# S5 convolution kernel products in four column groups of one PSUM bank, and their way to the Toeplitz matrices

## What is computed

```
dt = exp(log_dt);  a = exp(lambda*dt);  b' = ((a-1)/lambda) * b        # complex, per group and state
x[t] = a*x[t-1] + b' u[t]                                             # 512 tokens, an associative scan
y[t] = Re(c x[t]) + d_skip * u[t]
```

## Time and profile before

| what | value |
|---|---|
| median of 3 runs | 995.13 us (994.78 to 995.26) |
| the profiled execution, its own time | 994.91 us |
| span of its trace | 993.2 us |
| mean granted TensorE clock | 0.990 |

### The profile page before, as it was taken

One profiled execution on the slowest core, in us unless ns is written; L12 is line 12 of the kernel. 1 busy time (PEld: TensorE's weight loads), 2 busy tenths in 40 slices (PEclk: granted clock), 3 DMA queues, 4 the chain that ended last, 5 costly groups with the idle time before them and its releaser, 6 DMA issues.

```text
span 993.2 us, 14475 instructions
## 1 busy us (share of the span) xinstructions
PE 892.3 (90%) x4962; PEld 501.5 (50%) x4962; DVE 307.6 (31%) x812; ACT 173.9 (18%) x396; POOL 161.5 (16%) x260
## 2 busy tenths in 40 slices
PE   8999999999999999999979888988888887777865
PEld 3445876554444444445845555555555544343432
DVE  5990665761111111144731111111111111111117
ACT  1222148751000000100101111111111111111110
POOL 2010014430000000000022222222222222121210
PEclk9999999999999999999989999999999999999988
DMA  8342824029222220161799999999999999999555
GB/s 309 71 88 94 104 34 160 2 75 418 96 85 89 88 90 4 72 272 43 312 394 417 416 421 422 423 421 418 420 425 418 422 420 425 423 421 425 248 182 220
DMA packets 44553, 255.36 MB, mean 257 GB/s; under 512 B 15163, under 2 KB 15691, under 8 KB 28100
## 3 DMA queue, kind: packets, MB, share of 16 engines
q1 hardware_dynamic: 33988, 244.42, 62.2%
q0 software_dynamic: 10240, 9.64, 3.7%
q10 hardware_dynamic: 288, 0.81, 0.2%
HBM read 257.32 MB, written 21.04 MB: 280 GB/s over the span
## 4 chain that ended last, share of the span: by engine, by line
PE 63%; SPq 22%; DMA 6%; DVE 5%; issue 3%; ACT 1%; DVEq 0%; ACTq 0%; POOLq 0%
PE ps L665 19%; PE ps L804 9%; SPq L354 9%; SPq L347 8%; PE ps L443 6%; PE ps L701 6%; PE ps L824 5%; DMA reg_bo<-experts 4%; PE ps L435 3%; PE ps L622 2%; PE ps L578 2%; SPq L352 2%; PE ps L600 2%; PE ps L504 2%; SPq L411 1%
## 5 line engine op out<-in xcount | busy, mean ns | idle before, releaser
L804 PE MATMUL ps<-arena,reg_a 128*64 128x256 f32 x1024 | 118.2, 383 | 9.7 <-DMA arena<-experts 7.8
L1539 DVE TENSOR_TENSOR small<-reg_u,ps 128x128 f32<-128x128 f32 x62 | 17.9, 288 | 349.1 <-ACT reg_u L1050 349.1
L665 PE MATMUL ps<-xT,arena 128*128 128x512 f32 x256 | 111.2, 592 | 0.0
L804 PEld LDWEIGHTS ps<-arena,reg_a 128*64 128x64 f32 x1024 | 84.2, 138 | 52.4 <-issue 30.1
L1671 POOL DMA_INDIRECT ye_scratch<-reg_bo,reg_u x62 | 62.8, 1014 | 231.7 <-ACT reg_bo L1057 226.1
L665 PEld LDWEIGHTS ps<-xT,arena 128*128 128x128 f32 x256 | 48.6, 190 | 61.2 <-issue 61.2
L824 PE MATMUL ps<-arena,small 128*64 128x512 f32 x256 | 63.7, 616 | 13.8 <-DVE small L1546 13.0
L1057 ACT COPY reg_bo<-ps 128x512 f32<-128x512 f32 x62 | 36.4, 586 | 208.3 <-PE ps L824 208.3
L665 PE MATMUL ps<-reg_u,arena 128*128 128x512 f32 x128 | 57.5, 592 | 0.0
L701 PE MATMUL ps<-reg_a,reg_bo 128*128 128x512 f32 x128 | 55.8, 593 | 0.0
L443 PE MATMUL ps<-xT,reg_bo 128*128 128x512 f32 x128 | 55.7, 595 | 0.0
(11 more groups left out here) (277 smaller groups left out, 1155.7 us busy)
## 6 DMA issues: line engine op xcount, KB each, us to landing
arena<-experts SPq DMA_DIRECT2D x32, 2048.0 KB
arena<-experts SPq DMA_DIRECT2D x32, 1024.0 KB
reg_bo<-experts SPq DMA_DIRECT2D x8, 2048.0 KB
reg_a<-experts SPq DMA_DIRECT2D x8, 2048.0 KB
arena<-mid_w SPq DMA_DIRECT2D x8, 1792.0 KB, 7.4
xT<-experts SPq DMA_DIRECT2D x7, 2048.0 KB
x<-experts SPq DMA_DIRECT2D x7, 2048.0 KB
reg_bo<-experts SPq DMA_DIRECT2D x8, 1024.0 KB
```

The source lines that it names most:

```text
L665: m = pe.matmul(ps[bank][:, :], w[:, (o + c) * P:(o + c + 1) * P], rhs[:, c, :], start=(c == 0), stop=(c == nk - 1))
L804: m = pe.matmul(ps[2 + c % 2][64 * h:64 * h + 64, 0:DE], xgT[:, x, BLK * (c % 2):BLK * (c % 2 + 1)], gates[k][:, x * 512 + h * DE:x * 512 ...
```

## The change

The 16 pairs are taken four at a time (b = 0 to 3). The four pairs q = 0 to 3 of a batch write to partitions 32q to 32q+31 of bank 0, columns 128b to 128b+127, first the real parts of the four, then the imaginary parts. All 32 products end in one bank of 128 partitions by 512 columns. One count of s_kmm follows the last, ACT makes one copy to `kst`, now 128 partitions by 4 by 128, and DVE adds d_skip in a form of 128 partitions by 64 numbers, whose product is now made ahead of the wait. In `kst` each 16 partitions r hold the taps of groups r, r+8, r+16, r+24, so the taps go out by 8 transfers for each k, 64 in all, of 16 partitions times 4 groups.

```diff
-        kst = x1[0:32, 0:2048].rearrange("p (g n) -> p g n", g=GP)
+        kst = x1[:, 0:512].rearrange("p (b n) -> p b n", b=4)
...
-            sp_.wait_ge(s_kmm, 4)
+            sp_.wait_ge(s_kmm, 1)
...
-            sp_.wait_ge(s_kst, 5)
+            sp_.wait_ge(s_kst, 2)
             sp_.wait_ge(s_zero, 4)
             for k in range(T8):
-                for g2 in range(2):
-                    sp_.dma_start(toep[SH * k:SH * (k + 1), g2:SG:2, (T8 - 1 - k) * SH:P],
-                                  kst[SH * g2:SH * (g2 + 1), :, 0:(k + 1) * SH]).then_inc(s_toep, 16)
+                for r in range(8):
+                    sp_.dma_start(toep[SH * k:SH * (k + 1), r:SG:8, (T8 - 1 - k) * SH:P],
+                                  kst[SH * r:SH * (r + 1), :, 0:(k + 1) * SH]).then_inc(s_toep, 16)
...
-            for g in range(GP):
-                out = ps[g // 4][0:32, (g % 4) * P:(g % 4 + 1) * P]
-                pe.matmul(out, bbz[:, 0, g, :], ca_re[:, g, 0:8, :], start=True, stop=False)
-                m = pe.matmul(out, bbz[:, 1, g, :], ca_ni[:, g, 0:8, :], start=False, stop=True)
-                if g % 4 == 3:
-                    m.then_inc(s_kmm, 1)
+            for b in range(4):
+                for ri in range(2):
+                    for q in range(4):
+                        g = 4 * b + q
+                        m = pe.matmul(ps[0][32 * q:32 * q + 32, b * P:(b + 1) * P], bbz[:, ri, g, :], (ca_re, ca_ni)[ri][:, g, 0:8, :],
+                                      start=(b == 0 and ri == 0), stop=(ri == 1), skip_group_check=True)
+            m.then_inc(s_kmm, 1)
...
             pe.wait_ge(s_wv, 16)
+            pe.wait_ge(s_kst, 1)
             for t in range(TT):
-                pe.wait_ge(s_kst, t + 1)
...
-            pe.wait_ge(s_toep, 16 * 16)
+            pe.wait_ge(s_toep, 16 * 64)
...
-            for n in range(4):
-                act.wait_ge(s_kmm, n + 1)
-                act.copy(kst[:, 4 * n:4 * n + 4, :], ps[n][0:32, :].rearrange("p (q n) -> p q n", q=4)).then_inc(s_kst, 1)
+            act.wait_ge(s_kmm, 1)
+            act.copy(kst, ps[0][:, :].rearrange("p (b n) -> p b n", b=4)).then_inc(s_kst, 1)
...
-            dve.wait_ge(s_kst, 4)
-            sk = work[0:32, 0:256].rearrange("p (g h) -> p g h", g=GP)
-            link(tt(sk, s5d.unsqueeze(2).broadcast_to([32, GP, SH]), eyeh.unsqueeze(1).broadcast_to([32, GP, SH]), ALU.mult))
+            sk = work[:, 0:4 * SH].rearrange("p (b h) -> p b h", b=4)
+            link(tt(sk, s5d.unsqueeze(2).broadcast_to([P, 4, SH]), eyeh.unsqueeze(1).broadcast_to([P, 4, SH]), ALU.mult))
+            dve.wait_ge(s_kst, 1)
             dve.tensor_tensor(kst[:, :, 0:SH], kst[:, :, 0:SH], sk, ALU.add).then_inc(s_kst, 1)
-            dve.wait_ge(s_kst, 5)
+            dve.wait_ge(s_kst, 2)
```

More of the change, by code:

```diff
@@ L109, in build_kernel @@
         posb = sm.take(2 * 2 * SP2).rearrange("p (i g m) -> p i g m", i=2, g=2)
-        s5d = sm.take(GP, 32)
-        eyeh = sm.take(SH, 32)
+        s5d = sm.take(4)
+        eyeh = sm.take(SH)
         rtbl = sm.take(HEADS, 33)
@@ L1742, in pack @@
                          cm("s5_c_re"), cm("s5_c_im")], 1)
-    s5d = pair(f("s5_d")[0]).transpose(1, 2, 0).reshape(32, GP)
+    s5d = pair(f("s5_d")[0]).reshape(4, 4, 2, SH).transpose(1, 2, 3, 0).reshape(P, 4)
     dist = np.arange(-L, L)
@@ L1760, in pack @@
     experts = np.concatenate([gu, dn], 2).reshape(NE * P, EW)
-    eyeh = np.tile(np.eye(SH, dtype=np.float32), (2, 1))
+    eyeh = np.tile(np.eye(SH, dtype=np.float32), (8, 1))
     router = part(np.concatenate([f("router_w_group")[0], f("router_w_expert")[0]], 1))
```

## The result

The changed kernel takes 1005.15 us (median of 4 runs, 1004.42 to 1005.87) against 994.95 us of the kernel before in the same session: ratio 1.0103, 95% interval 1.0085 to 1.012. It is slower by 10.2 us, where 5.3 us less was forecast. The profiled execution took 1005.87 us.

The account below looks back on a forecast made before the run. TensorE, busy 90% of the span, was taken to bound the kernel around the change. 994.91 us of the profiled execution - 5.3 for the tap products, no other term, gave 989.6, so 989.8 for the runs; range 988.8 to 992.4.

Parts of the forecast that it names:

- The bound and the place: Tap products, 7.10 us, lie on TensorE's chain; only the Toeplitz filling ahead of L524 could arrive late.
- Part 1: Tap products on TensorE, four column groups side by side: 1.8 us instead of 7.10, term -5.3 us.
- Parts 2 and 3: Fewer ACT copies and a smaller DVE addition, then biasT transfers starting at 99.2, 4.9 us earlier: no term.
- Part 4: 64 tap transfers on SP's queue, 0.385 us apart, land at 133.0; TensorE asks at 134.8, so hidden.
- The backlog: SP's queue stalls behind biasT's packets; with the limit counted in pieces, 25 new transfers are out by 114.8 us.
- rival A's second form: Tap transfers late: backlog counts transfers, about 8 ahead, landing at 139.7; 994.5 us, no change; chance 0.05.
- Rival C: Each tap transfer on SP's queue costs an old one's 0.655 us; TensorE waits 13 us, 1002.6 us; chance 0.06.
- Rival D: Gain given back later by the clock, at its lower level in stretch 500 to 510; total loss, chance 0.03.
- The rule of the Trainium skill: Put small transfers together; at 2.0 us each, 64 in sequence take 128 us, kernel near 1088 us.

Follow-up runs that it names:

- the version with 16 transfers: The changed kernel with its column groups kept, but four copies and the old 16 tap transfers put back; 990.9 us, ratio 0.9944 to the kernel before.

## Why the prediction was wrong

- **The bound and the place.** Right: the tap products lay on the chain, and the filling of the Toeplitz matrices was the one thing that could arrive late.
- **Part 1.** Right: 1.88 us against 1.8, L496 at 98.76 against 98.7. All of the 5.3 us reaches `ssm_out` in the version with 16 transfers, 134.81 against the 134.8 forecast.
- **Parts 2 and 3.** Right: one copy of 0.59 us, the addition 0.23 us, both hidden; L329 starts at 99.29 against 99.2, L336 at 103.06 against 103.0.
- **Part 4: this step failed.** It put the pace of the 64 transfers at 0.385 us, by a straight line through L329 (432 ns, 128 pieces) and L336 (610 ns, 256 pieces), and so read the difference between the two as the cost of pieces. It is a difference between two kinds of transfer: L322 and L329 read DRAM, L336 moves inside SBUF. The changed kernel's own shape took 426 ns from DRAM and 598 inside SBUF. The runs showed 595 ns at 64 pieces, 602 at 128 and some 615 at 256 where nothing holds the issue: about 0.64 us with the gap. Nor did pieces set L322 apart from L329: 8 partitions from DRAM took 301 ns with 32 pieces and 298 with 8. The one row of the right kind, L336 itself, gave 0.65 us, and stood in the text as the far end of the range, not as the value. Two smaller terms were off: a small transfer lands 1.8 to 2.0 us after its issue and not 3.6, and the slack before the change was 7.0 us and not 8, since the last transfer, issued at 127.9, landed 5.2 us later, and TensorE came at 140.1.
- **The backlog.** 25 transfers were to be out by 114.8, the rest at the queue's pace. Only 17 were out by then: at 0.64 us apart there is room for 18 from 103.06. The three long stalls of the earlier trace rows are gone; the longest issues are 1.89 and 1.92 us. The trace speaks against the count of transfers in rival A's second form, which had SP stop about 8 ahead: at 118.3 us 17 of the new transfers were issued and had not landed. That the limit counts pieces isn't shown by this. It didn't matter for the time.
- **Rival C** was the mechanism: 41.9 us of issues from 103.0, landing at 148, a wait of 13 us, 1002.6 us. Measured: 43.98 us, 148.55, 13.59 us. It was given only 0.06 because of L322's 299 ns, which are of the other kind. Its sum lacked the lower clock behind the wait (1.8 us); with it, it would have been 1004.4.
- **Rival D**, the clock: it didn't cost the gain where it was sought, but the new idle time brought a new stretch at the lower level, which no term had.
- **The rule of the Trainium skill** on many small transfers (DMA: Bandwidth & Descriptors, Rules for kernel authors) was right in its direction for these transfers. This case's number for it is the 0.6 us that SP needs for each, not the 2.0 us of the page's other section, since transfers overlap once issued (1.8 us from issue to landing here at the least, with 0.64 us between two starts).

## What to carry to other kernels

Count the transfers on a queue before their bytes, and price one from a row with the same source and destination memories; if there is only one such row, its value is the forecast and not the bound. When a stage is moved ahead, list what feeds its next consumer and sum that queue's issues from their new start: here 32 transfers fit under 32 us of cover and 64 did not. Packing small products into column groups was worth its 5.3 us at `ssm_out`, and 4.4 us of the time with 16 transfers (6.3 with 32, where other sessions' shifts of a microsecond are of the same size); two or four shifted copies on an idle engine kept the transfers few.

## What the runs showed of the hardware that was not expected

- Inside SBUF, transfers with 1, 4, 8 or 16 pieces a row for 16 partitions took 586, 598, 602 and some 615 ns to issue; with 8 and 4 partitions they took more, 710 and 671 ns. From DRAM to SBUF 8 partitions took less than 16, 0.30 against 0.43 us.
- Two issuing engines at once kept 617 and 604 ns each: this cost isn't shared between queues.
- After 13.6 us in which TensorE stood still, its clock was at the lower level for the first 4 us of work (0.50 granted in 148 to 152 us). Keeping it busy with products took that away in the trace (3.68 to 1.96 us), but not from the median (1004.37 against 1004.3 us).
- The versions that gain 5.3 us at 135 us of the span scatter more from run to run than the kernel before: 2.9 us (988.55 to 991.41) over five executions of the version with 16 transfers, against 0.9 (994.87 to 995.73) over nine. Its trace is 5.3 us ahead at 499 us and 3.5 at the end, the loss falling in the experts' stage after 780 us and behind it. What sets this wasn't tried.
